# Start-up loads of a hybrid decoder step on one core: gains and the first pair of x ahead, constants and indexer pages held until the fourth weight chunk

## The reference, cut to what matters

```python
h = rms_norm(x, norm1_g)
u, q, k, v, iq, ik, iw = project(h, pos, w_in, ...)     # h @ w_in, 1024 x 1864, then norm and rotary
ya, state = pool_mix(u, ...)
yb = attend(q, k, v, iq, ik, iw)                        # indexer scores -> top k -> attention
x = x + concat([ya, yb]) @ w_o
x = x + peer(rms_norm(x, norm2_g), w_pq, sub_keys, expert_u, expert_v)

# attend for the sample tokens:
past_ik = cache_ik[page_table].reshape(DB, P, IDX_DIM)  # 8 sequences x 8 pages of indexer keys
s = einsum('bqhd,bld->bqhl', iq, concat([past_ik, ik]))
score = einsum('bqhl,bqh->bql', relu(s), iw)
```

## Time and profile before

| what | value |
|---|---|
| median of 3 runs | 1041.75 us (1040.34 to 1044.41) |
| time of the profiled execution | 1040.79 us |
| its span, first to last instruction | 1039.1 us |
| PE busy in the span | 1018.1 us (98%) |
| first matmul starts | 10.66 us into the span |
| granted TensorE clock, mean | 0.998 of full |

### The profile page before, as it was taken

How to read it: one execution, slowest core, us unless ns; L and a number is a source line. 1 busy time by engine, 2 the same in 40 slices (tenths; PEclk the granted TensorE clock), 3 DMA queues, 4 the chain that set the end, 5 groups by cost and what they waited for, 6 DMA issues and landing times.

```text
span 1039.1 us, 18875 instructions
## 1 busy us (share of the span) xinstructions
PE 1018.1 (98%) x6303; PEld 848.5 (82%) x6303; DVE 716.8 (69%) x1510; ACT 519.2 (50%) x1083; POOL 452.7 (44%) x329
## 2 busy tenths in 40 slices
PE   5999999999999999999999999999999999999998
PEld 2447878889999999999999988888878887778886
DVE  2559989649999728787888876764555555555553
ACT  2123222343445567777777775644444454444542
POOL 4653443245688878778887771011111111111110
PEclk9999999999999999999999999999999999999999
DMA  9434469358755578888888876675666766676662
GB/s 341 114 122 158 151 203 337 119 203 292 268 177 183 171 236 286 287 279 289 287 292 272 288 232 226 230 270 194 228 224 235 240 228 223 227 239 234 228 227 100
DMA packets 79439, 237.39 MB, mean 228 GB/s; under 512 B 11749, under 2 KB 23661, under 8 KB 78980
## 3 DMA queue, kind: packets, MB, share of 16 engines
q1 hardware_dynamic: 65052, 195.51, 55.4%
q0 software_dynamic: 13040, 40.52, 12.2%
q10 hardware_dynamic: 1280, 0.53, 0.2%
HBM read 233.56 MB, written 3.14 MB: 228 GB/s over the span
## 4 chain that ended last, share of the span: by engine, by line
PE 80%; DVE 9%; issue 4%; POOL 3%; ACTq 2%; DMA 1%; ACT 0%; SPq 0%; POOLq 0%; DVEq 0%
PE psum L1058 33%; PE psum L988 14%; PE psum L993 10%; PE psum L992 6%; PE psum L1004 5%; POOL w_lo L1521 3%; DVE top L1625 3%; DVE work_s L1626 2%; PE psum L580 2%; PE psum L819 2%; PE psum L1089 2%; PE psum L792 1%; ACTq L366 1%; ACTq L363 1%; PE psum L762 1%
## 5 line engine op out<-in xcount | busy, mean ns | idle before, releaser
L1521 POOL TENSOR_TENSOR w_lo<-w_raw,w_hi 128x1024 fp32r<-128x1024 f32 x116 | 285.6, 2467 | 95.1 <-ACT w_hi L1110 92.2
L1110 ACT ACTIVATE w_hi<-w_raw 128x1024 fp32r<-128x1024 f32 x214 | 227.4, 1063 | 175.6 <-PE psum L1058 95.4
L993 PE MATMUL psum<-h_split,w_lo 128*128 128x256 f32 x1024 | 287.6, 281 | 0.0
L988 PE MATMUL psum<-h_split,w_hi 128*128 128x512 f32 x640 | 232.1, 403 | 0.0
L993 PEld LDWEIGHTS psum<-h_split,w_lo 128*128 128x128 f32 x1024 | 194.6, 190 | 0.0
L1549 POOL DMA_INDIRECT rows_in<-expert_v,eidx x32 | 45.5, 1421 | 329.6 <-PE psum L1089 317.6
L1877 DVE TENSOR_TENSOR w_lo<-w_raw,w_hi 128x1024 fp32r<-128x1024 f32 x98 | 120.1, 1225 | 78.5 <-ACT w_hi L1110 78.5
L1058 PE MATMUL psum<-w_hi,ag_hi 128*128 128x512 f32 x512 | 160.1, 394 | 0.3 <-DVE ag_lo L1884 0.3
L1058 PE MATMUL psum<-w_hi,ag_lo 128*128 128x512 f32 x512 | 158.2, 390 | 0.0
L992 PE MATMUL psum<-h_split,w_hi 128*128 128x256 f32 x768 | 140.4, 285 | 1.3 <-issue 0.9
L988 PEld LDWEIGHTS psum<-h_split,w_hi 128*128 128x128 f32 x640 | 120.4, 188 | 25.5
(11 more groups left out here) (294 smaller groups left out, 1413.6 us busy)
## 6 DMA issues: line engine op xcount, KB each, us to landing
w_raw<-expert_ut SPq DMA_DIRECT2D x128, 512.0 KB, 4.7
w_raw<-expert_v SPq DMA_DIRECT2D x86, 512.0 KB, 3.9
raw_more<-expert_v SPq DMA_DIRECT2D x42, 512.0 KB, 4.1
w_slice<-w_pq_cols SPq DMA_DIRECT2D x32, 512.0 KB, 6.2
rows_in<-h_save SPq DMA_DIRECT2D x32, 512.0 KB, 4.5
w_most<-w_in_blocks SPq DMA_DIRECT2D x8, 699.0 KB, 12.3
w_slice<-w_o_half SPq DMA_DIRECT2D x8, 512.0 KB, 4.3
v_cache<-cache_v POOLq DMA_DIRECT2D x64, 64.0 KB, 2.9
```

What stands on the lines that cost most here:

```text
L988: pe.matmul(psum[:, 2 + s, :], w_hi[:, s, c, :], h_split[:, c].rearrange("p a t -> p (a t)"), start=(c == 0), stop=False, skip_group_check ...
L993: mm = pe.matmul(out, w_lo[:, s, c, :], h_split[:, c, 0], start=False, stop=(c == KC - 1), skip_group_check=wide)
L1110: return act.activation(out, in_, ACT.Copy)
L1521: pool.tensor_tensor(w_lo[:, s], w_raw[:, s], w_hi[:, s].bitcast(F32), ALU.subtract).then_inc(S["w_lo_ready"], 1)
```

## The change

Four things move or are added; no transfer and no arithmetic is added or taken away.

- SP issues the first pair of x, then weight chunk 0, then the other three pairs of x, then chunks 1 to 7, and `ident` last.
- POOL issues the norm scales ahead of the page table.
- POOL waits, before the seven constants and so before its 24 pages, until chunk 3 of the weights is in.
- ACT waits for the same before its 16 pages.

```diff
--- before.py
+++ after.py
@@ -343,7 +343,7 @@
     assert DOT_AT[-1] < G_END and ROW_AT[-1] < LAST - 5
     assert G_AT % RING == 0 and G_END % RING == 0 and G_END <= NU - RING
     v_rows = expert_v.rearrange("a (n p) d -> (a n) p d", p=P)
-    gain_loads = [(pages[0:1, :], page_table.rearrange("b n -> (b n)").unsqueeze(0)), (gains[:, :], gain_cols)]
+    gain_loads = [(gains[:, :], gain_cols), (pages[0:1, :], page_table.rearrange("b n -> (b n)").unsqueeze(0))]
     early_loads = [
         (rope[0:NS, 2, :], c_rope[SEQ:NT, :]), (rope[:, 0:2, :], c_rope[0:SEQ, :].rearrange("(t p) c -> p t c", p=P)),
         (fold[:], c_fold), (causal_new[:], c_causal_new), (own[:], c_own), (iota[:], c_iota),
@@ -409,12 +409,17 @@
         @block.sync
         def _(sp):
 
-            for k in range(0, KC, 2):
+            def load_x(k):
                 sp.dma_start(xT[:, k:k + 2, :], x_t[:, k:k + 2, :]).then_inc(S[f"x_in{k // 2}"], 16)
-            sp.dma_start(ident[:], c_ident).then_inc(S["ident_in"], 16)
+
+            load_x(0)
             for k in range(KC):
                 sp.dma_start(w_most[:, k], w_in_blocks[k, :, 0:3, :]).then_inc(S[f"w_in_in{k}"], 16)
                 sp.dma_start(w_rest[:, k], w_in_blocks[k, :, 3, :]).then_inc(S[f"w_in_in{k}"], 16)
+                if k == 0:
+                    for c in range(2, KC, 2):
+                        load_x(c)
+            sp.dma_start(ident[:], c_ident).then_inc(S["ident_in"], 16)
             sp.wait_ge(S["gains_in"], 16 * len(gain_loads))
             ik_loads(sp, 0, W_IK[0])
             sp.dma_start(keysT[:], keys_t).then_inc(S["keys_in"], 16)
@@ -1117,6 +1122,7 @@
             act.activation(rstd_a[:, 0:12], rstd_b[:, 0:12], ACT.Sqrt).then_inc(S["rstd_root"], 1)
 
             act.wait_ge(S["gains_in"], 16 * len(gain_loads))
+            act.wait_ge(S["w_in_in3"], 32)
             ik_loads(act, W_IK[0] + W_IK[1], W_IK[2])
 
             def head_root(i, n):
@@ -1456,6 +1462,7 @@
             pool.memset(ones[:, :], 1.0).then_inc(S["ones_set"], 1)
             for dst, src in gain_loads:
                 pool.dma_start(dst, src).then_inc(S["gains_in"], 16)
+            pool.wait_ge(S["w_in_in3"], 32)
             for dst, src in early_loads:
                 pool.dma_start(dst, src).then_inc(S["consts_in"], 16)
             pool.wait_ge(S["gains_in"], 16 * len(gain_loads))
```

## The result

The changed kernel takes 1051.74 us (median of 4 runs, 1050.94 to 1052.94) against 1041.05 for the kernel before (4 runs): a ratio of 1.010, 95% interval 1.008 to 1.012, or 10.7 us. The forecast was 1053.0 in 1049.0 to 1057.5, as a sum of +11.4 us on a median of 1041.75; with the fourth run the median of before is 0.7 lower. The profiled execution took 1051.94 us with a span of 1050.3, 11.2 longer than the span of before.

The account below looks back on a forecast made before the run. PE's one long stream was taken to bound the kernel: +10.1 us waiting for POOL and +1.3 for the clock, +11.4 on a median of 1041.75, make 1053 us, range 1049 to 1057.5.

Parts of the forecast that it names:

- The mechanism: POOL's wait delays its pages and rotary, so PE idles some 12 us before its transposes and turns `fold_iw` 10.1 us later.
- When chunk 3 is in: Weight chunk 3, which POOL and ACT wait for, lands at 15.7 us instead of about 17.9, bounds 14.5 and 18.0.
- POOL's stream: Behind POOL's wait, 3.89 us of constants and 32.9 us to the rotary, which starts at 52.5 in place of 39.85.
- Rotary and `fold_iw`: POOL's indexer rotary takes 5.3 us and `fold_iw` adds 0.86, so PE can turn it at 58.7 instead of 48.64.
- PE's early start: PE starts near 6.7, 4 us earlier, but the wait for POOL swallows all of the gain: 0 us.
- ACT: ACT's pages wait until 15.7, `copy_z` comes at 38.8; ACT and DVE off the path, worth -0.8 us without POOL.
- The clock: After its new gap PE restarts at a lower clock: +1.3 us, bounded by 0 and 1.94.
- What was given back: After 48.6 every stage hangs on PE and its later waits are 1.1 us at the longest: nothing is made good.
- That issuing pages is cheap: Rival: POOL's register work overlaps issuing, its 24 pages need 12.4 us, and the time is 1041; chance 0.04.

Follow-up runs that it names:

- the one with chunk 1: The whole change, but POOL waits for weight chunk 1 in place of chunk 3: 1047.23 us, ratio 1.005.
- fixed pages: The whole change, with POOL's 24 pages taken from fixed physical pages, without loop, table loads and register work: 1042.11 us, ratio 1.0012.
- PE kept busy: The whole change with 14 more products on PE, results overwritten later, in the gap before the transposes: 1048.77 us, ratio 1.0076.
- four units ahead: The whole change with the last four prompt units of the input projection put ahead of PE's transposes: 1057.3 us, ratio 1.0151.
- the reordering alone: The whole change without POOL's and ACT's waits for chunk 3, only the new order of transfers: 1041.31 us, ratio 1.0002.
- one unit ahead: The change without either wait, and prompt unit 4 of the input projection put ahead of PE's transposes: 1044.81 us, ratio 1.003.
- the split on the whole change: The whole change with half of the third group of output-projection products moved ahead of PE's 1.1 us wait for ACT: 1049.55 us, ratio 1.0082.

## Why the prediction was right, step by step

**The mechanism** was POOL's stream, and the run without POOL's wait, the one with that wait alone and the one with chunk 1 each show it. The gap, its place and its releaser were as forecast: 12.57 us ahead of line 563 for POOL's line 1490, forecast some 12.

**When chunk 3 is in.** Forecast 15.7, and POOL's constants began at 17.07: 1.4 too early. By the chain that ended last chunk 3 landed at 16.79. The term took a count of bytes for a landing: I had 5.0 MB up to chunk 3, and the SP queue had moved 5.23 MB by 15.7 and 5.70 by 16.8, so part of the chunks behind it was moved before chunk 3 was whole. POOL started at 16.1 to 16.4 in the runs without ACT's wait, with fixed pages, with PE kept busy and with four units ahead, so part of it is spread. Still inside 14.5 to 18.0.

**POOL's stream.** Forecast 3.9 + 32.9 = 36.8 us from the first constant to the rotary; measured 35.59 (17.07 to 52.66), since the first page period opened with 2.50 us of idle and not 3.97. This error is the opposite of the last one, and the rotary started at 52.66 for a forecast of 52.5. The agreement to 0.2 us is luck in part.

**Rotary and `fold_iw`.** 4.9 and 0.8 us for 5.3 and 0.9. The shift on PE came to +10.02 for +10.1.

**PE's early start.** First product at 7.69, forecast 6.7: the page table, now issued second, lands at 7.25 and DVE waits for both. PE then waited 1.05 us for the sums of squares, which I had not seen. It was worth nothing, as forecast, and the reordering alone confirms it.

**ACT.** Its first copy came at 39.53, to the hundredth where it was before, forecast 38.8: the late chunk again. I had the earlier copy as worth 0.8 us if POOL were not there; by the run without POOL's wait against the one with the reordering alone, ACT's wait is a loss of some 2 us that POOL hides.

**The clock.** +1.3 forecast, +1.57 measured from `fold_iw` to the scores (5.11 against 3.54), and the run with PE kept busy shows that it is the clock. The rule of the Trainium skill (TensorE: Matmul & The Clock Gate, section on the HAM clock gate) that an idle array drops to 1.2 GHz held after every gap of PE of 2.6 us or more behind the start in these traces; the sum by it, +12.0, was further off than mine, and the next term is missing from both.

**What was given back.** I put it at nothing. It was 1.66 us in the profiled executions: the fall of the clock at 116 to 121, which I had read as a fixed part of the kernel, does not occur in that of the changed one. It is no property of the kernel before either, by the mean clocks above. The tail from line 792/797 to the end took 910.8 us before and 912.1 after, 1.3 more, within the 910.5 to 912.4 of the other profiled runs; nothing here explains it. The span's sum is 10.02 + 1.57 - 1.66 + 1.3 = 11.2 for a forecast of 11.4. The first two terms were right by their mechanism; that the last two nearly cancel is luck, and by the medians the change cost 10.7.

**The rivals.** That issuing pages is cheap failed as the kernel stands. The Trainium skill (DMA: Bandwidth & Descriptors, section Issuing engines are not separate DMA queues) calls the issue time usually small relative to the DMA itself; for pages whose address is read from a table the trace does not agree, since POOL spends 1.2 us on each of them and a page lands 2.4 us after its issue (median of the 24). The fixed pages mark the rival's condition: without the register work the 24 issues took 12.38 us (forecast 12.4), and the time was 1042.11 (forecast 1041), not to be told from no loss.

## What to carry to other kernels

Holding a transfer back holds back all that stands behind it in the issuing engine's stream. Before a wait goes in, add up what the engine still has to do until somebody needs it, registers and issuing included, and compare that with the slack; here 35.6 us of constants and pages (17.07 to 52.66) stood ahead of a rotary whose result had 1.2 us of slack.

A wait for an early input is no gain to be booked until every stream that meets at the next common point has been timed: PE, POOL, ACT and SP all met at 47 to 52 us, so 3 us at the start were worth nothing that could be measured.

Work moved into PE's waits can save more than the waits, where it keeps the clock up: 3.4 us for waits of 1.9 between two profiled executions, 1.9 by the medians. One profile of a kernel is one execution; look at the mean clock of the others before a fall seen in it is counted as part of the kernel.

## What the hardware showed that I had not expected

The same two waits of PE, 1.14 and 0.72 us, were followed by a fall of the clock in two profiled executions and left it at 1.00 in eight others, the one with one unit ahead among them. Each fall seen there cost 1.66 to 1.68 us. That the kernels' earlier course decides it isn't shown: executions of one and the same kernel, the one before, differ in their mean clock, 0.999 or more in 17 and less in 12. What decides it was not tried.

After the gap the loss between `fold_iw` and the scores was not the same from run to run either: 1.6 us in the whole change (5.11 against 3.54), 2.0 without ACT's wait (57.69 to 63.28), 2.5 with chunk 1 (53.10 to 59.19), 3.1 with the split on the whole change (57.94 to 64.56), though the gap was 6.9 us with chunk 1 and over 12 in the others. After the much shorter wait of 2.6 us, without POOL's wait, it was 1.7 (50.45 to 55.68).

One page with its address from a table costs POOL 29.1 / 24 = 1.2 us and one with a fixed address 12.38 / 24 = 0.52. In both forms the transfer itself is 32 KB, so the 0.7 us of difference are spent on the sequencer and not on the bytes.
